# Down weights of the expert layers issued from ScalarE's queue in place of SyncE's

## The reference, cut to what matters

```python
e_v, e_i = lax.top_k(e_sel, MOE_TOPK)              # MOE_TOPK = 2
gate = jax.nn.softmax(e_v, axis=-1) * g_p
hid = jax.nn.silu(jnp.einsum('nd,edf->nef', x, w_g)) * jnp.einsum('nd,edf->nef', x, w_u)
hid = hid * combine[:, :, None]
y = hid.reshape(B * T, N_EXPERTS * D_EXPERT) @ w_d.reshape(N_EXPERTS * D_EXPERT, D)
```

## Time and profile before

| | us |
|---|---|
| median of three runs | 1044.03 |
| profiled execution | 1044.46 |
| its span | 1042.3 |
| TensorE (PE) busy | 932.8 (89%) |
| VectorE (DVE) busy | 462.1 (44%) |
| ScalarE (ACT) busy | 226.7 (22%) |
| GpSimd (POOL) busy | 106.9 (10%) |

### The profile page before, as it was taken

One profiled execution on the slowest core, in us unless ns is written; L12 is line 12 of the kernel. 1 busy time (PEld: TensorE's weight loads), 2 busy tenths in 40 slices (PEclk: granted clock), 3 DMA queues, 4 the chain that ended last, 5 costly groups with the idle time before them and its releaser, 6 DMA issues.

```text
span 1042.3 us, 11963 instructions
## 1 busy us (share of the span) xinstructions
PE 932.8 (89%) x4160; PEld 469.1 (45%) x4160; DVE 462.1 (44%) x1035; ACT 226.7 (22%) x460; POOL 106.9 (10%) x165
## 2 busy tenths in 40 slices
PE   2799999999989999999988997899799999999980
PEld 0455454645343444444433465445444444545430
DVE  1157633244433444444554365624334444444454
ACT  2223132212211211211222114311111112111111
POOL 2300011300210000000001101020010000000002
PEclk9899999899989999999998999999699999999995
DMA  9992350947899999999996543021599999999921
GB/s 304 362 348 81 123 182 30 373 157 288 333 366 420 420 421 420 419 421 421 415 379 245 183 161 132 0 87 41 204 419 419 420 420 421 421 420 419 416 83 60
DMA packets 76135, 303.59 MB, mean 291 GB/s; under 512 B 9593, under 2 KB 9905, under 8 KB 50632
## 3 DMA queue, kind: packets, MB, share of 16 engines
q1 hardware_dynamic: 66504, 281.28, 68.1%
q0 software_dynamic: 8320, 17.18, 4.9%
q10 hardware_dynamic: 1280, 4.72, 1.2%
HBM read 309.75 MB, written 5.32 MB: 302 GB/s over the span
## 4 chain that ended last, share of the span: by engine, by line
PE 70%; DMA 15%; DVE 6%; issue 3%; ACT 3%; SPq 2%; POOL 0%; POOLq 0%; DVEq 0%; ACTq 0%
PE psum L1024 17%; PE psum L705 16%; DMA ring<-in_w_exp_up 11%; PE psum L1050 7%; PE psum L777 4%; PE psum L903 4%; PE psum L729 4%; PE psum L998 2%; DVE ht L1797 2%; DMA ring<-in_w_mod 2%; DMA arena<-h_rows,arena 2%; PE psum L1012 2%; PE psum L1013 1%; PE psum L978 1%; PE psum L951 1%
## 5 line engine op out<-in xcount | busy, mean ns | idle before, releaser
L1024 PE MATMUL psum<-ring,arena 128*64 128x512 f32 x1024 | 226.7, 594 | 8.4 <-DMA ring<-in_w_exp_up 6.6
L705 PE MATMUL psum<-ring,ht 128*128 128x512 f32 (+1 forms) x432 | 170.5, 552 | 3.4 <-ACT ht L1225 2.7
L1024 PEld LDWEIGHTS psum<-ring,arena 128*64 128x64 f32 x1024 | 85.1, 137 | 146.6 <-issue 142.0
L1050 PE MATMUL psum<-ring,arena 128*64 128x512 f32 x512 | 116.9, 599 | 8.3 <-DVE ht L1797 7.2
L705 PEld LDWEIGHTS psum<-ring,ht 128*128 128x128 f32 x432 | 81.5, 192 | 85.7 <-issue 77.3
L1797 DVE TENSOR_TENSOR ht<-ht,psum 128x512 f32<-128x512 f32 x172 | 105.5, 682 | 4.1 <-PE psum L1013 2.0
L1840 DVE TENSOR_TENSOR arena<-arena,psum 128x256 f32<-128x256 f32 x32 | 13.5, 422 | 172.5 <-ACT arena L1368 172.5
L1375 ACT ACTIVATE y_top<-psum,arena 128x512 fp32r<-128x512 f32 x64 | 44.0, 687 | 183.7 <-PE psum L1050 183.7
L1012 PE MATMUL psum<-y_top,to_token 128*128 128x512 f32 x192 | 80.3, 418 | 3.5 <-DVE y_low L1828 3.5
L1828 DVE SCALAR_TENSOR_TENSOR y_low<-psum,arena,y_top 128x512 fp32r<-128x512 f32 x64 | 48.0, 751 | 79.2 <-ACT y_top L1375 79.2
L1013 PE MATMUL psum<-y_low,to_token 128*128 128x512 f32 x192 | 76.9, 401 | 0.0
(11 more groups left out here) (301 smaller groups left out, 899.5 us busy)
## 6 DMA issues: line engine op xcount, KB each, us to landing
ring<-in_w_exp_gate SPq DMA_DIRECT2D x32, 2048.0 KB, 18.0
ring<-in_w_exp_up SPq DMA_DIRECT2D x32, 2048.0 KB, 23.0
ring<-in_w_exp_down SPq DMA_DIRECT2D x32, 2048.0 KB, 20.5
ring<-in_w_mod SPq DMA_DIRECT2D x24, 2048.0 KB, 15.1
ring<-in_w_in_even SPq DMA_DIRECT2D x5, 2048.0 KB, 19.9
ring<-in_w_in_odd SPq DMA_DIRECT2D x3, 2048.0 KB, 19.6
ring<-in_w_out_even SPq DMA_DIRECT2D x2, 2048.0 KB, 8.5
shift_scale<-mod_rows POOLq DMA_DIRECT2D x2, 2048.0 KB, 10.1
```

Of the source, the lines that this page charges most:

```text
L705: mm = pe.matmul(psum[:, to, 0:cols], HT[:, b, k, :], w[:, k, :], start=(k == 0), stop=(k == KC - 1))
L1024: mm = pe.matmul(psum[64 * e:64 * e + 64, 2, :], XT[:, k, 64 * e:64 * e + 64], RG[:, 3 * v:3 * v + 2, e, k, :], start=(k == 0), stop=(k == ...
L1050: mm = pe.matmul(psum[64 * e:64 * e + 64, 4 + n, :], HTS[v][:, k, 64 * e:64 * e + 64], RD[:, 3 * v + 2, e, k, n * 512:(n + 1) * 512], star ...
```

## The change

For pairs 2 to 15, the load of down(j) leaves SyncE's program and goes to ScalarE's, on ScalarE's DMA queue. There it stands behind ScalarE's wait for the second half of down(j-2), ahead of the second half of y_top of that pair. Gate and up stay where they are, and so do the loads of pairs 0 and 1. On SyncE the wait for down(j-2) falls away. ScalarE's loop is one turn shorter, and the last two pairs, which load nothing, stand behind it.

```diff
@@ SyncE, experts
                         first_expert = sp.snap(((i * 2 + u) % PAIRS) * 2)
                         multiplied = sp.snap(i * 2 + (u - 1))
-                        down_multiplied = sp.snap(i * 4 + (2 * u - 2))
                         sp.wait_ge(S(f"moe{l}_gate_up"), multiplied)
                         sp.sem_inc(S("slots_freed"), 1)
                         load_experts(l, 0, first_expert, 3 * u)
                         load_experts(l, 1, first_expert, 3 * u + 1)
-                        sp.wait_ge(S(f"moe{l}_down"), down_multiplied)
-                        sp.sem_inc(S("slots_freed"), 1)
-                        load_experts(l, 2, first_expert, 3 * u + 2)
@@ ScalarE, experts
-                def pair(q, v, first=False, second=False):
+                down_weights = d["w_exp_down"][l].rearrange("e (p k) n -> p e (k n)", p=P)
+
+                def pair(q, v, first=False, second=False, next_expert=None):
                     act.wait_ge(M("gate_up"), q + 1)
...
                         act.wait_ge(M("down"), q * 2 + n + 1)
                         if not first and n == 0:
                             act.wait_ge(M("back_ps"), q * 6)
+                        if n == 1 and next_expert is not None:
+                            act.dma_start(RS[:, 3 * v + 2], down_weights[:, bass.ds(next_expert, 2), :]).then_inc(M(f"in_{3 * v + 2}"), 16)
                         act.activation(Y_HI[:, n * 512:(n + 1) * 512], bank(4 + n), ACT.Copy, scale=token[v][:, 1:2]).then_inc(M("y_top"), 1)
...
-                pair(0, 0, first=True)
-                pair(1, 1, second=True)
+                pair(0, 0, first=True, next_expert=4)
+                pair(1, 1, second=True, next_expert=6)
                 R = rounds_of(act, l)
-                with act.Fori(1, R * (PAIRS // 2)) as i:
+                with act.Fori(1, R * (PAIRS // 2) - 1) as i:
                     for v in range(2):
-                        pair(i * 2 + v, v)
+                        pair(i * 2 + v, v, next_expert=act.snap(((i * 2 + (v + 2)) % PAIRS) * 2))
+                for v in range(2):
+                    pair(R * PAIRS + (v - 2), v)
```

## The result

The changed kernel takes 1053.22 us (median of six runs, 1049.90 to 1055.48), the kernel before 1043.99 us in the same comparison. The ratio is 1.0088, with a 95% interval of 1.0069 to 1.0107: slower by 9.2 us. The profiled execution is the quickest of the six, 1049.90 us.

A forecast was written before the change was run, and what follows sets the result against it. Nearly full DMA engines and TensorE bound the kernel, with up weights landing just in time. 4.6 us in layer 0 plus 4.4 in layer 1 make 9.0; 1044.46 + 9.0 - 0.43 = 1053.0 us, range 1045.5 to 1059.

The forecast's parts named there:

- What bounds the kernel: Expert stages: weights set 15.59 us a pair, TensorE alone needs about 15.2; any later landing of up is paid in full.
- SyncE's 28 waits and issues at 0, ScalarE's 28 issues at 0: Expert stages: SyncE losing 28 waits and issues, and ScalarE gaining 28 issues ahead of y_top's second half, each change the time by 0.
- the cover that the prediction named: ScalarE's pair: some 5.6 us by which an added issue may delay y_top before any work that needs it is late.
- Share of one half, down ahead of up: Expert stages: down's queue gets half the transfers, so down(j) lands 10 us after issue, ahead of up(j), which lands 5.0 us later.
- the case of one third: Expert stages: if down's queue got one third of the transfers, down(j) and up(j) would land together.
- Layer 0, by DMA +4.6, layer 1 +4.4: Start of gate_up(15): up(15) lands one load later, adding 4.6 us in layer 0 and 4.4 in layer 1.
- Layer 0, by TensorE: up(2) at 326.4, ten us late: Layer 0: down(2) and down(3) both pass up(2), gate_up(2) starts at 326.8, and 13 pairs of 15.17 us end at 524.0.
- Gathers and the next stage's chunks at 0: GpSimd's gathers land at 479.4 at most, before use at 480.11; next stage's chunks have the same bytes ahead: 0 each.
- order of issue holds across queues: Rival, 13%: both queues' descriptors are worked off in order of issue, down lands where it did, 1044.0, not slower.
- the new queue gets little: Rival, 6%: at a 16% share a down load needs 32 us, TensorE waits up to 8.1 us per layer, up to 1069.
- Two queues do not fill the engines better: Rival, 7%, claimed the opposite: two queues raise the rate in the expert stages, TensorE would bind, 1044.0 to 1046.5.
- ScalarE isn't held up: Rival, 4%, claimed the opposite: ScalarE's issue is refused beyond 5.6 us, one us over costs 28, 1065 and more.

The follow-up runs named there:

- rows_late: Kernel before, with SyncE's loads of rows needed only after the experts issued behind the last weights: 1034.79 us against 1043.64, ratio 0.9920.
- first_two: Only down(2) and down(3) of each layer issued by ScalarE, the other 12 by SyncE as before: 1046.08 us against 1043.71 for the kernel before, ratio 1.0018.
- tiny: Kernel before, plus a useless 4 KB load issued by ScalarE 28 times where the change issues down weights: 1045.86 us against 1043.64, ratio 1.0014.
- change_again: The changed kernel as it is, run once more on another chip against the kernel before: 1055.59 us against 1044.12, ratio 1.0120.
- last_two: Only down(14) and down(15) of each layer issued by ScalarE, the other 12 by SyncE as before: 1060.14 us against 1043.64 for the kernel before, ratio 1.0170.

## Why the prediction was right, point by point

**What bounds the kernel**: held for a delay of all the loads that follow, and rows_late is the same statement read from the other end. That whatever makes up land later is paid in full was too strong: in first_two up(2) comes 5 us later in layer 0, as in the change, and of the delays in both layers 1.9 us are left.

**SyncE's 28 waits and issues at 0, ScalarE's 28 issues at 0**: held. The issue took 0.39 us where I had 0.33 from the store, and tiny shows no cost that can be told from none. I had also said that no one would wait longer for y_top; VectorE did, by 17.7 us in all, inside the cover that the prediction named.

**Share of one half, down ahead of up**: the order held; its sizes were off. A down lands 14.0 us after its issue, not 10 to 12, and 1.5 us ahead of its up, not 5. The share while both move is a half over the whole load (2.10 to 2.09 MB); what I had left out are the first 3.4 us, in which the new queue gets nothing. With 14 us it comes close to the case of one third, where both land together, and the cost is the same one load.

**Layer 0, by DMA +4.6, layer 1 +4.4**: +4.84 and +4.66 in the trace, 9.2 us in the medians. That the sum came out so close is in part luck. On another chip the same two kernels are 1.2% apart (change_again), some 12.5 us. And in layer 1 of this trace gate_up(0) took 8.76 us, 1.7 more than before, at a mean granted clock of 0.81; it took 8.78 in tiny, too, where the weights come in the old order.

```profile
759.31 8.76 PE psum L1020 x32
```

So the 4.66 isn't the change's alone.

**Layer 0, by TensorE: up(2) at 326.4, ten us late**: wrong. It landed 5.0 us late. The step that failed is that down(3) would meet up(2) still under way and go ahead of it as well. down(3) is issued at 313.54 us in the trace after, 3.8 us before up(2) lands, and with a late start of some 3.5 us it moves its first packets when up(2) is all but in. The issue itself came later, too, 25.2 us after that of up(2) instead of 22.8, since TensorE had waited 2.5 us longer for the rows of pair 2. On another chip (change_again) up(2) took 31.1 us, 7 us late: there down(3) was issued 22.9 us after up(2), and about half of it (1.06 MB from 320.5 to 325.2 us) did come ahead. That both of my ways met at 524 was luck in one of them: TensorE's way had a delay too large by 5 us.

Something that the prediction did not have worked against that. After the longer wait gate_up(2) took 9.39 us instead of 7.10; the window of its matmuls has a mean granted clock of 0.75, so that part of it ran at 1.2 GHz, the lower of the two levels, after TensorE had stood still for 4.2 us:

```profile
317.70:327.10 9.40, 9.40 (x33) 3.13 (x33) 0.00 (x0) 0.00 (x0) 0.00 (x0) 0.75 1.01 421
```

In the change this doesn't reach the end: the next pairs find their weights landed and take 15.0 to 15.2 us, until the weights set the pace again, and so win it back. In last_two, with one pair to go, it is paid: 9.28 us in layer 0 and 8.61 in layer 1.

**Gathers and the next stage's chunks at 0**: 0 was right, but not because gathers landed early enough. Their median is 8.2 us as before; those at the start of a layer land later, and TensorE waits 3.7 us more for them in all. In layer 0 up(2) comes later still and covers it. Behind the experts the chain has nothing new.

**The rivals**: that order of issue holds across queues, and that the new queue gets little, are both refuted by the packets above. Two queues do not fill the engines better, 418 GB/s against 420; there the trace agrees with the Trainium skill ("DMA: Bandwidth & Descriptors", section "Issuing engines are not separate DMA queues"), by which transfers run on the same 16 DMA engines whichever engine started them. ScalarE isn't held up; its price of 1065 doesn't follow from 28 us for each us over, which make 1072.

## What to carry to other kernels

Here, with the DMA engines full, a second queue brought no bandwidth; it changed who is served first. Before a load goes to another queue, write down which transfer the busiest engine waits for and what is served ahead of it, before and after: here a load that newly passed cost its own time, 5 us, once, as long as the loads behind it kept the new order; where they went back to the old one (first_two), most of it was caught up. The same list read backwards finds gains: here the rows that no one needs until the stage is over stood ahead of the first weights, and moving them behind the last was worth 0.8%.

## What the runs showed of the hardware that was not expected

A transfer on a queue that was empty starts late when another queue has the engines full: some 3.5 us from issue to first packet (nothing of down(12) in 3.4 us, nothing of the load of 4 KB in 3.4), and 6.9 us from issue to landing for 4 KB. With the engines idle the same queue starts sooner. A store of the kernel before, with nothing else moving, has packets within 1.2 us of its issue; the second line is of 716.6 to 717 us.

```profile
715.78 0.33 ACTq L1337 DMA_DIRECT2D h_rows<-h  x1
...
q10 hardware_dynamic: 40, 0.16, 101.0%
```

Then the queues move packets in like numbers, whatever their size (35 packets of one to 34 of the other, at 0.57 and 0.28 MB), though not in every window of 2 us (70 to 36). Why the start is late is open; no run here was made for it.
